# Earlier first gathers, row sums between the query projections, and smaller last batches in a two-layer kernel on one core

## The reference, cut to what matters

```python
q = (xb @ w_q).reshape(PEER_BLOCK, PEER_HEADS, 2, PEER_HALF)
s = jnp.einsum('thpd,hpnd->thpn', q, sub_keys)
s_top, i_top = lax.top_k(s, PEER_TOPK)               # 16 of 128, both halves of 8 heads
cand = s_top[:, :, 0, :, None] + s_top[:, :, 1, None, :]
best, pos = lax.top_k(cand, PEER_TOPK)               # 16 experts of each head
g = jax.nn.softmax(best, axis=-1)
act = jax.nn.gelu(jnp.einsum('td,thkd->thk', xb, u[expert]), approximate=False)
return jnp.einsum('thk,thkd->td', (g * act), v[expert])
```

## Time and profile before

| what | value |
|---|---|
| median of three runs | 1284.71 us |
| the profiled execution | 1285.52 us, span 1283.8 us |
| mean granted TensorE clock | 0.94 |
| PE, DVE, ACT, POOL busy | 87%, 61%, 36%, 23% of the span |
| gathers (queue q0) | 36864 packets, 268.45 MB |
| other loads (queue q1) | 24448 packets, 94.48 MB |
| HBM, mean over the span | 283 GB/s |

### The profile page before, as it was taken

One profiled execution on the slowest core, in us unless ns is written; L12 is line 12 of the kernel. 1 busy time (PEld: TensorE's weight loads), 2 busy tenths in 40 slices (PEclk: granted clock), 3 DMA queues, 4 the chain that ended last, 5 costly groups with the idle time before them and its releaser, 6 DMA issues.

```text
span 1283.8 us, 13226 instructions
## 1 busy us (share of the span) xinstructions
PE 1112.9 (87%) x4936; PEld 746.5 (58%) x4936; DVE 778.8 (61%) x1528; ACT 466.1 (36%) x979; POOL 298.7 (23%) x313
## 2 busy tenths in 40 slices
PE   9999999689786877868768687786999999999997
PEld 9888878544332332323323232232898989888886
DVE  6597527445747658476584764444694655665575
ACT  5657221222222223222232222222457434574443
POOL 1054102134344342533425332231001000000001
PEclk9999999799888897988979889888999999999999
DMA  5543347689999999999999999987244332544623
GB/s 205 195 166 134 121 151 279 270 348 421 405 422 420 423 422 420 422 421 421 422 420 422 421 422 422 410 352 290 98 165 164 132 113 93 191 148 157 230 90 114
DMA packets 61841, 363.98 MB, mean 284 GB/s; under 512 B 6848, under 2 KB 17360, under 8 KB 20304
## 3 DMA queue, kind: packets, MB, share of 16 engines
q0 software_dynamic: 36864, 268.45, 50.5%
q1 hardware_dynamic: 24448, 94.48, 20.8%
q10 hardware_dynamic: 464, 0.20, 0.1%
HBM read 361.01 MB, written 2.10 MB: 283 GB/s over the span
## 4 chain that ended last, share of the span: by engine, by line
PE 60%; DMA 19%; DVE 12%; ACT 4%; issue 3%; POOL 2%; POOLq 0%; DVEq 0%; SPq 0%; ACTq 0%
PE ps L2054 19%; PE ps L1890 19%; PE ps L1856 9%; DMA ring<-in_uv,big 8%; DMA big<-in_uv,big 7%; PE ps L1823 3%; DMA past_actT<-in_uv,big 3%; PE ps L1941 2%; DMA ring<-in_peer_w_q 2%; DVE ring L1469 1%; ACT big L985 1%; DVE lo L1264 1%; PE ps L2004 1%; DVE big L1469 1%; POOL big L770 1%
## 5 line engine op out<-in xcount | busy, mean ns | idle before, releaser
L2054 PE MATMUL ps<-big 128*128 128x512 f32 x552 | 274.0, 647 | 67.5 <-ACT big L985 64.7
L1469 DVE CUSTOM_DVE_ANT_0 big<-big,ps 128x1024 f32<-128x1024 f32 x138 | 167.0, 1220 | 147.1 <-DMA big<-in_uv,big 145.8
L2054 PEld LDWEIGHTS ps<-big 128*128 128x128 f32 x552 | 112.6, 207 | 220.6 <-issue 141.3
L1890 PE MATMUL ps<-hi,x 128*128 128x512 f32 x704 | 224.8, 393 | 1.2 <-DVE lo L1264 1.0
L2054 PE MATMUL ps<-ring,big 128*128 128x512 f32 x336 | 167.6, 642 | 52.4 <-ACT big L985 49.5
L770 POOL DMA_INDIRECT big<-in_uv,big x138 | 132.2, 958 | 271.7 <-PE ps L2054 172.0
L1264 DVE TENSOR_TENSOR lo<-raw,hi 128x2048 fp32r<-128x2048 f32 x60 | 139.2, 2321 | 71.5 <-ACT hi L851 71.2
L977 ACT ACTIVATE big<-big 128x4 f32<-128x4 f32 x64 | 13.1, 205 | 446.5 <-DVE big L1469 440.2
L2054 PEld LDWEIGHTS ps<-ring,big 128*128 128x128 f32 x336 | 68.7, 208 | 146.0 <-issue 88.1
L1890 PEld LDWEIGHTS ps<-hi,x 128*128 128x128 f32 x704 | 132.2, 188 | 29.6 <-issue 2.3
L1469 DVE CUSTOM_DVE_ANT_0 ring<-ring,ps 128x1024 f32<-128x1024 f32 x84 | 101.5, 1220 | 76.0 <-DMA ring<-in_uv,big 74.8
(11 more groups left out here) (369 smaller groups left out, 1344.5 us busy)
## 6 DMA issues: line engine op xcount, KB each, us to landing
raw<-in_pieces SPq DMA_DIRECT2D x61, 1024.0 KB, 4.8
ring<-in_peer_w_q SPq DMA_DIRECT2D x8, 1024.0 KB, 5.5
big<-in_up SPq DMA_DIRECT2D x4, 2048.0 KB, 8.5
big<-in_uv,big POOLq DMA_INDIRECT x138, 21.2
ring<-in_w_mem_kv SPq DMA_DIRECT2D x2, 1024.0 KB, 5.2
ring<-in_uv,big POOLq DMA_INDIRECT x84
resid<-in_x SPq DMA_DIRECT2D x2, 512.0 KB, 4.9
raw<-in_pieces SPq DMA_DIRECT2D x2, 512.0 KB, 9.0
```

What stands on the lines that cost most here:

```text
L1469: ins = dve.tensor_tensor_reduce(out=row, in0=row, in1=hn_ps[n], scale=1.0, scalar=0.0, op0=ALU.mult, op1=ALU.add, accum_out=dots[:, n, s: ...
L1890: ins = pe.matmul(o, a, b[:, c], start=(s == 0 and c == 0 and k == 0), stop=(s == 1 and c == HALF - 1 and k == 2))
L2054: ins = pe.matmul(ps[:, 4 + 2 * n + half, :], diag[:, s % DIAGS], row_home[home_of[k]][:, D + half * TILE:D + (half + 1) * TILE], start=(s ...
```

## The change

What it does, part by part:

1. `search` takes a head count. The first step is head 0 alone, the second head 1; units of two heads follow. The three wide operations over 2 x 32 x 16 numbers become two each. The indices of row 0 are there after head 0; row 16 waits for head 1.
2. The queries no longer keep 4096 columns but share a ring of three heads (1536 columns), so that the place of query1 is free at row 7. `mixT` takes row 8, and its memory weights (w_mem columns 256 to 511) are loaded after it, behind batch 2, instead of in the stage before. Nine homes are thus open to rows 0 to 8: early0 to early3, ring3 to ring5, query1, mixT. After that mixT is closed until row 48, and ring2, actT, query0, keys open at rows 13, 22, 23, 24, memT, ring0, ring1 at 56, 56, 57, mkv at 62.
3. Batches 0 to 2 are weighed by ScalarE and summed by TensorE between the query groups (after heads 4, 5 and 6). The memory steps move from between the query groups, and from batches 2 to 7, to behind batches 4 to 11, four steps each.
4. VectorE: softmax(0) and the dots of rows 4 to 7 come ahead of the search of unit 1, rows 8 to 31 behind it.
5. In the last 32 rows query0 and query1 stay open: 12 homes. `norm_f` is loaded into `gain_row`, as soon as that is used up, in place of the room behind the queries.
6. The last four rows are batches of 2, 1 and 1 rows.
7. Tile 0's sum, product with norm_f, squares, inverse roots and scaling move into the second tile's rows (`add_peer(0)`, `normed(0)`, `squares(0)`, `mean_square(0)`, `inverse_rms(0)`, `scale_rows(0)`), and the split of dnq0 goes ahead of the last six rows. 20 fillers instead of 22.

```diff
-BATCHES = ROWS // BATCH
-UNIT_BATCHES = PICKS // BATCH
+BATCH_ENDS = [*range(BATCH, ROWS - BATCH + 1, BATCH), ROWS - 2, ROWS - 1, ROWS]
+BATCHES = len(BATCH_ENDS)
+BATCHES_0 = SLOTS // BATCH
+SPLIT_BATCH = SLOTS // BATCH * NT - 2
...
-        FIRST_ROW = {"early0": 0, "early1": 0, "early2": 0, "early3": 0, "ring3": 4, "ring4": 5, "ring5": 6, "ring2": 7,
-                     "actT": 8, "query0": 9, "query1": 10, "keys": 11, "mixT": 24, "memT": 40, "ring0": 40, "ring1": 41, "mkv": 48}
+        FIRST_ROW = {"early0": 0, "early1": 0, "early2": 0, "early3": 0, "ring3": 4, "ring4": 5, "ring5": 6, "query1": 7, "mixT": 8,
+                     "ring2": 13, "actT": 22, "query0": 23, "keys": 24, "memT": 56, "ring0": 56, "ring1": 57, "mkv": 62}
+        WEIGHTS_IN_MIXT = range(9, 48)
-        KEPT_FREE = ("ring0", "ring1", "ring2", "ring4", "query0", "query1", "mixT")
+        KEPT_FREE = ("ring0", "ring1", "ring2", "ring4", "mixT")
...
+            sp.wait_ge(v_done, batch_of(rows_in["mixT"][0]) + 1)
+            sp.wait_ge(cols_then_mem_loaded, 80)
+            sp.dma_start(mixT, w_mem[:, :, T:2 * T]).then_inc(cols_then_mem_loaded, 16)
...
+                if k == PICKS * (UNITS - 2):
+                    inverse_rms(0)
+                if k == TOP:
+                    pool.wait_ge(idx_done, 2)
...
             for i in range(PH):
                 out_query(i)
-                if i == 3:
+                if i == 2:
                     exponentials(0)
                 if i >= 3:
                     out_scores(i - 1)
+                    if i < PH - 1:
+                        weigh(i - 3)
...
-            search(0)
-            search(1)
-            for u in range(UNITS):
+            search(0, 0, 1, 0)
+            search(0, 1, 1, 1)
+            dot_rows(0, BATCH)
+            softmax(0)
+            dot_rows(BATCH, 2 * BATCH)
+            search_unit(1)
+            dot_rows(2 * BATCH, PICKS)
+            search_unit(2)
+            for u in range(1, UNITS):
                 softmax(u)
...
+                if u == UNITS // 2:
+                    dot_rows(PICKS * u, PICKS * u + TOP)
+                    add_peer(0)
+                    normed(0)
+                    dot_rows(PICKS * u + TOP, PICKS * u + PICKS)
+                    mean_square(0)
...
             for i in range(PH):
                 query_features(i)
+                if i == 0:
+                    pe.wait_ge(cols_then_mem_loaded, 80)
                 if i < 2:
-                    memory(19 + 2 * i, 21 + 2 * i)
-                    if i == 0:
-                        pe.wait_ge(cols_then_mem_loaded, 96)
                     key_scores(i)
                 elif i > 2:
                     key_scores(i - 1)
-            memory(23, 25)
+                if 4 <= i < PH - 1:
+                    weighted_rows(i - 4)
             key_scores(PH - 1)
-            for b in range(BATCHES):
+            for b in range(PH - 5, BATCHES):
                 weighted_rows(b)
-                if b == 2:
-                    memory(25, 28)
-                if 3 <= b < 8:
-                    memory(4 * b + 16, 4 * b + 20)
-
-            keep_busy(3, 22)
+                if 4 <= b < 12:
+                    memory(4 * b, 4 * b + 4)
+
+            keep_busy(3, 20)
```

More of the change, by code:

```diff
@@ L82, with batch_of, rows_of @@
 PIECES += [f"out{_h}{_s}" for _h in range(2) for _s in range(2)]
+def batch_of(k):
+    return next(b for b, end in enumerate(BATCH_ENDS) if k < end)
+def rows_of(b):
+    return range(BATCH_ENDS[b - 1] if b else 0, BATCH_ENDS[b])
 def bcast(ap, dim, n):
@@ L766, in _ @@
                 if earlier:
-                    pool.wait_ge(v_done, earlier[-1] // BATCH + 1)
+                    pool.wait_ge(v_done, batch_of(earlier[-1]) + 1)
+                    if name == "mixT" and len(earlier) == 1:
+                        pool.wait_ge(group_done, group_no["mk1"] + 1)
                 elif name in home_ready:
@@ new lines, in search, with search_unit @@
+                wait_marked()
+                for a in range(2):
+                    mark(dve.tensor_reduce(key[:, a, 0:m], pick[:, a, 0:m], AX.X, ALU.add))
+                wait_marked()
+                link(dve.scalar_tensor_tensor(idxf[:, 0:m], key[:, 0, 0:m], float(NKEY), key[:, 1, 0:m], ALU.mult, ALU.add))
+                dve.tensor_copy(idx[:, n, TOP * h0:TOP * h0 + m], idxf[:, 0:m]).then_inc(idx_done, 1)
+            def search_unit(u):
+                n, r = unit_of(u)
+                search(n, 2 * r, 2, u + 1)
@@ L1504, in _ @@
-            for n in range(NT):
-                one = slice(n, n + 1)
-                dve.wait_ge(rstd_done, 6 + n)
-                dve.tensor_scalar(scaled2[:, n], scaled2[:, n], rstd_x[:, one], None, ALU.mult).then_inc(scaled_done, 1)
-            dve.wait_ge(piece_hi, piece_no["dnq0"] + 1)
-            dve.tensor_tensor(lo2[:, 0, D:2 * D], raw2[:, 0, D:2 * D], hi2[:, 0, D:2 * D].bitcast(F32), ALU.subtract).then_inc(piece_lo, 1)
+                    dve.tensor_tensor(hn_ps[1], scaled_p[:, 1], gain_row, ALU.mult).then_inc(gain_loaded_then_used, 1)
@@ L2033, in _ @@
                     memory(14, 16)
-            memory(16, 19)
             for k in range(2):
@@ L2050, in weighted_rows @@
                 pe.wait_ge(diag_done, b + 1)
-                for k in range(BATCH * b, BATCH * b + BATCH):
+                for k in rows_of(b):
                     n, s = k // SLOTS, k % SLOTS
```

236 lines of the change are left out of this document (130 added, 106 removed).

## The result

| | before | after |
|---|---|---|
| median | 1283.24 us (4 runs) | 1267.84 us (4 runs, 1267.1 to 1271.57) |
| span of the profiled execution | 1283.8 us | 1269.8 us (1271.57 us in all) |
| mean DMA rate over the span | 283 GB/s | 287 GB/s |

The ratio is 0.9869, 95% interval [0.9846, 0.9892]: faster. The forecast was 1267, its range 1255 to 1278. The profiled execution of after was the slowest of its four, 3.7 us above the median; all that follows compares its span with that of before, a difference of 14.0 us.

The account below looks back on a forecast made before the run. The prediction took the DMA gather stream as the bound: 256 rows at 2.49 us, 637 us. Terms -8 - 5 - 5 = -18 against the profiled 1285.5 us gave 1267.5, stated as 1267, range 1255 to 1278.

Parts of the forecast that it names:

- the sum of -18: Whole kernel: -8 (start), -5 (last 32 rows) and -5 (behind the last row, norm included), against the profiled 1285.5 us.
- A, the first gather: Start of the gather stream: one-head search issues the first gather at 188.9 instead of 205.1, 16.2 us earlier.
- A, the part that reaches row 63: Early rows: with 18.7 us idle and two more loads in the stream, 6.4 to 9.8 us gained, taken as -8.
- A page's rule: Query 5's weights: an earlier trace row gave landing after 24.9 us and a 2.6 us wait; the sum assumed no wait.
- query weights come last: Rival at the query stage: TensorE waits for query weights, 3 to 7 us less gained, 1272; chance 0.06.
- B, the last 32 rows: Last 32 rows: 12 homes instead of 10 cut 6.8 us idle to 1.8, -5 (0 to -6).
- C, behind the last row: Last dot to TensorE's end: small last batches end at L+8 to L+9.5 instead of 13.4 us, -4.5 (bounds -8, -2).
- Norm: Behind the last batch: one tile's second product no longer stands before the last square and root, -0.5, at most 1.2.
- Homes last: Rival in the early rows: TensorE isn't late, 10.5 us idle behind 265 go, 28 in all, 1257; chance 0.19.
- Given back: Rival in the early rows: another 8 us idle, start gains nothing, last-rows and end gains remain, 1277; chance 0.13.
- Slower by a low clock: Rival at batches 4 to 11: TensorE stays at 1.2 GHz, 4 us each costs 32, 1299; chance 0.07.

Follow-up runs that it names:

- e1: Changed kernel with the first search step covering two heads again instead of one: 1280.8 us, ratio 0.9949 to the kernel before.
- e9: Changed kernel with weighing and row sums of batches 0 to 2 put back behind all queries: 1303.8 us, ratio 1.013 to the kernel before.
- e7: Changed kernel with the gathers of rows 6 to 8 held until query 5's weights landed: 1274.3 us, ratio 0.9904 to the kernel before.
- e8: Changed kernel with query 5's weights replaced by other 1 MB data in 8 KB runs instead of 1 KB: 1266.1 us (one run, before 1285.9).
- e3: Changed kernel with query0 and query1 closed in the last 32 rows, 10 homes instead of 12: 1274.8 us, ratio 0.9903 to the kernel before.
- e4: Changed kernel with the load of piece dnk0 held back until the last dot: 1271.4 us, ratio 0.9881 to the kernel before.
- the control: The changed kernel once more, unedited (after_again): median 1273.4 us over all five executions, ratio 0.9881 to the kernel before.
- e2: Changed kernel with a last batch of four rows instead of 2, 1, 1: 1277.15 us, ratio 0.9924 to the kernel before.
- e12: Changed kernel with tile 0's norm put back to the end, beside tile 1's: 1275.1 us, ratio 0.9887 to the kernel before.
- e13: e10 plus the load of dnk0 held until the last dot and 20 filler products behind each of batches 57 to 61: 1276.5 us, ratio 0.9909.
- e14: e13 with 10 filler products instead of 20 behind each of batches 57 to 61: 1267.2 us, ratio 0.9862 to the kernel before.
- e10: Changed kernel with sixteen memory steps behind batch 7, four behind batch 8, and some homes opened earlier: 1267.3 us, ratio 0.9861 to the kernel before.

## Why the prediction was right, and by which steps

The total was right (1267 against 1267.84), closer than its parts: their sizes are off in both directions, and that they cancel is luck. Against the profiled executions, for which the sum of -18 was made, it was 4 us too hopeful (-14.0); the medians differ by 15.4 us, or 16.9 against the 1284.71 shown ahead of the prediction.

**A, the first gather: right.** 189.93 against 188.9. The parts: query 0 at 170.83 (170.5), scores at 178.78 (178.2), the search from 180.57 to 189.44 and so 8.9 us (8.6). e1 shows what it is worth: without it 9 to 10 of the 15 us are gone by the ratios, 11 at the last dot. It does not carry the change alone, as e9 shows.

**A, the part that reaches row 63: -6.2 against -8.** Row 61's dot came at 387.28; the sum had 384 without and 387.4 with the 3.4 us by which the same sum fell short in before, and I took the middle. The shortfall was there again: the first 41 us of the stream moved 368 and 399 GB/s at a full share, against 421 later. Taking less than all of it is the step that failed. Part of the low rate is the query weights: where e7 leaves them alone with the engines (210 to 216 us), 1 KB runs move 348 GB/s at a share of 1.09. The 3.4 us themselves hold a slip: the sum for before lets the data flow at 205.4, 0.3 us behind the issue, that for after 1.5 us behind it. With 1.5 in both, the shortfall is 2.1 us and the whole of it would have given 386.1. Beneath, two errors offset each other. The holes came where they were forecast: rows 14, 18 and 21 at 237.38, 252.05 and 268.62 (232, 248, 264.8), row 44 at 332.64 (328.3). They start 4 to 5 us later than forecast throughout. TensorE waited 2.45 us for query 5's weights, which landed 24.84 us after 195.60: the 24.9 and the 2.6 that stood in "A page's rule", worked out from the earlier trace rows, and which I gave 0.06 as the rival *query weights come last*. As a fact it came true, though not as the place last in line that the figure was worked out from: by 217 us the load had moved 0.88 of its 1.05 MB, and the rest followed when the nine gathers ran out. As a rival it was priced at 3 to 7 us, and e8, which removes it, gives 3.8 us at the last dot. To it belongs that query 5 itself then ran 8.86 us instead of 6.9. So "the sum above has no such wait" was wrong as well. Against that, of the 18.7 us idle that I summed, about 15.7 came (the shares short of 1 in each microsecond from 206 to 380 us).

**B, the last 32 rows: nothing against -5.** The step "hence the 6.8 us idle ... I leave 1.8" took idle time for time. Up to row 251 the stream's idle time did fall. The two holes of before, by stretches of 5 us:

```profile
835.00:840.00 5.00, 3.29 (x8) 1.14 (x6) 2.37 (x5) 1.90 (x8) 1.13 (x2) 1.00 0.68 284
860.00:865.00 5.00, 4.91 (x12) 2.01 (x11) 2.43 (x4) 1.14 (x4) 2.82 (x3) 1.00 0.58 200
```

They are 3.7 us idle together; in after there are 0.89 and 0.93 in the stretches from 865 to 875, 0.9 us. But row 63's dot to row 251's took 481.0 us against 481.7. The DMA view says where the rest went: in these stretches the gather queue moved 197.9 MB in after and 196.9 before, nearly a row more in 0.6 us less. From row 251's dot to the last dot it then moved 2.89 MB against 3.44: 0.55 MB more of the last four rows was under way by then, 1.3 us at 421 GB/s. The other 0.4 MB are a difference at row 63's end. Rows 252 to 255 should have had the benefit (before: 11.9 us from row 251 to the last dot; four rows are 9.96), but there the load of dnk0 put in 2.5 us. The prediction named the early split of dnq0 and costed its 2.4 us of VectorE; it did not follow the split to the buffer that it frees and the load that this triggers. e3 shows that the homes themselves do what was claimed of them: 3 to 4 us by the ratios, 6.4 at the last dot of its profile. With ten homes in both, this stretch took 500.8 us in e3 and 493.5 before; of these 7.3 us the load of dnk0 explains some 2.5, and the rest is open.

**C, behind the last row: -6.5 against -4.5.** The same 2.5 us with the other sign. TensorE's end hangs on row 251, not on the last row, so a last dot that is held back by dnk0 makes the stretch behind it shorter and the end no later; e4 takes the load away and gains nothing. Counted from row 251's dot, TensorE ends after 19.3 us, against 25.2 before: 5.9 us, for which my steps (9.96 to the last dot, then 8 to 9.5) gave 18.0 to 19.5. B and C together were forecast at -9.5 and gave -6.5; what is missing is mostly the -3.1 up to row 251 (B without the 1.9 us in the last four rows), of which 0.6 came. Part of the size is the clock of one execution: in the control, with batch 62 warm, TensorE ends 5.3 us behind the last dot and 17.7 behind row 251's. e2 confirms the small batches, 13.0 against 6.9 us.

**Norm: -1.3 against -0.5**, just beyond my bound of 1.2; e12 repeats 6.8 and 5.5 us. The half of the second product (2.35 to 1.2) is 1.1 of it, as I had it; I had taken 0.5 because the squares might set the end, and they don't.

**The rivals.** *Homes last* (0.19): no, 15.7 us idle stood in the stream. *Given back* (0.13): no, 9 to 10 us of the early start arrive (e1). Its price had a slip: B, C and the norm without A are 10 us, which gives 1275 and not 1277. *Slower by a low clock* (0.07): batches 5 and 8 ran cold (322.85, one row 3.78 us), but the clock came back within two rows and no batch behind it lost more than a few microseconds. The change can be slower for another reason, though: e9 shows that with the sums of batches 0 to 2 left out of the query groups it is, by 1.3%.

**The page's rule.** I set the rule of the Trainium skill (DMA: Bandwidth & Descriptors, section Queues, rings and completion order), round-robin between queues at packet granularity, against the row of 21.80 us and wrote that the row doesn't look so. That was a wrong reading of both. While a query load was under way, the dots of rows 3 to 7 came 2.91 us apart (205.49, 208.40, 211.33 ...) instead of 2.49: the load had a seventh of the engines' time (14.7%) and an eighth of the bytes, not the half that equal turns of equal pieces would give, and not nothing, as it would as last in line. From 205 to 217 us each queue moved 596 packets. By turns of one piece each, with pieces of 1 KB against 8, a small share is what the rule gives, so the trace agrees with it once the size of the pieces is counted, if the profile's packets are what takes turns. A strict ninth of the bytes (1 in 9) would be 2.80 us a row; a gathered row has 144 packets (36864 over 256 rows), 128 of them of 8 KB, so that the load takes 144 KB beside each row.

## What to carry to other kernels

Price a freed buffer by what it lets start: an operation moved earlier on a busy stretch brings its successor's load with it, and only the row on which the end hangs (here row 251, not the last) tells whether that load costs. Where an early start leans on few buffers, the step that gives them back has to move with it; half of such a change (e9) can be worse than none. And between two DMA streams look at the run length of each before you assume equal shares.

## What the runs showed of the hardware that I had not expected

A 1 MB load in 1 KB runs beside gathers in 8 KB runs takes 24.8 to 28.4 us from issue to landing (the fastest of the same kind of load in after 5.3), and slows the gathers only from 2.49 to 2.91 us a row; both queues move the same number of packets. In 8 KB runs it lands in 10.3 us and takes half the bytes while it flows (e8). Filler products in float32 (128 columns) are two records each and take 0.223 us in all, so 20 of them are 4.46 us (e13) and 10 are 2.23 (e14). With ten of them behind each of five batches the granted clock was 1.00 to the end (e14), where e10 without them was granted 0.50 and 0.54 in 840 to 845 and 870 to 875; but the control was granted 1.00 from 835 to 886 without any filler, where after, the same program, had 0.90. So the clock of the last batches differs between executions of one program, and one profile each does not show what fillers do to it; e14's span is 1.6 us below e10's, its ratio the same.
